# Scaling by the norm after the up projection, and an earlier split of y for w_out, in a float32 block kernel on one core

## The reference

```python
x = x + y                                    # y = concat(...) @ w_o
uf = causal_dwconv(rmsnorm(x, g_ffn[i]) @ w_up[i], w_ffn_conv[i])   # 3 taps over tokens
gate, up = jnp.split(uf, 2, axis=-1)
x = x + (jax.nn.silu(gate) * up) @ w_down[i]

def rmsnorm(x, g):                           # per token t: one factor r[t], per feature: g
    return x * rsqrt(mean(x * x) + 1e-6) * g
```

```python
proj = rms_norm(x, g) @ w_in_2               # q, k, v and gates of the four groups
y = concat(fox, diff, moba, gla) * silu(gates)
x = x + y @ w_out_2
```

## Time and profile before

| | us |
|---|---|
| median of 3 runs | 3679.07 (3676.93 to 3680.88) |
| the profiled execution, its own time | 3682.81 |
| its span, first to last instruction | 3681.0 |
| PE busy in it | 3506.0 (95%) |
| DVE busy | 2588.7 (70%) |
| ACT busy | 1524.9 (41%) |
| POOL busy | 971.7 (26%) |

### The profile page before, as it was taken

How to read it: one execution, slowest core, us unless ns; L and a number is a source line. 1 busy time by engine, 2 the same in 40 slices (tenths; PEclk the granted TensorE clock), 3 DMA queues, 4 the chain that set the end, 5 groups by cost and what they waited for, 6 DMA issues and landing times. The chain is left out here.

```text
span 3681.0 us, 56972 instructions
## 1 busy us (share of the span) xinstructions
PE 3506.0 (95%) x21706; PEld 3093.1 (84%) x21706; DVE 2588.7 (70%) x3400; ACT 1524.9 (41%) x1581; POOL 971.7 (26%) x793
## 2 busy tenths in 40 slices
PE   8988989999999999888899999999999999999998
PEld 7977878888888889877788888888888888878887
DVE  7587577767676765676677676767766866677765
ACT  4432444333433544333444343335444443444442
POOL 3082422212021430553322030313422003140004
PEclk9998999999999999989999999999999999999999
DMA  5332445555555544323455555555543444443443
GB/s 219 138 122 88 152 156 183 174 203 179 198 180 188 190 163 164 133 77 129 150 193 188 188 193 184 193 176 190 177 166 127 150 171 171 166 149 132 155 167 141
DMA packets 93808, 604.06 MB, mean 164 GB/s; under 512 B 10416, under 2 KB 13649, under 8 KB 33105
## 3 DMA queue, kind: packets, MB, share of 16 engines
q1 hardware_dynamic: 92736, 598.78, 46.6%
q10 hardware_dynamic: 912, 3.12, 0.2%
HBM read 599.76 MB, written 2.10 MB: 164 GB/s over the span
## 5 line engine op out<-in xcount | busy, mean ns | idle before, releaser
L531 PE MATMUL bank<-H,whi 128*128 128x512 f32 x6304 | 2247.5, 401 | 44.6 <-DVE H L1444 19.0
L535 PE MATMUL bank<-H,wlo 128*128 128x256 f32 x7552 | 2140.3, 283 | 0.0
L970 ACT ACTIVATE whi<-raw 128x2048 fp32r<-128x2048 f32 (+4 forms) x636 | 1098.5, 1728 | 1180.0 <-DMA raw<-in_slabs_down 274.2
L1364 DVE TENSOR_TENSOR wlo<-raw,whi 128x2048 fp32r<-128x2048 f32 (+4 forms) x636 | 1339.8, 2107 | 250.0 <-ACT whi L970 246.7
L531 PEld LDWEIGHTS bank<-H,whi 128*128 128x128 f32 x6304 | 1192.3, 189 | 343.8 <-issue 37.2
L535 PEld LDWEIGHTS bank<-H,wlo 128*128 128x128 f32 x7552 | 1451.2, 192 | 0.3
L531 PE MATMUL bank<-G,whi 128*128 128x512 f32 x1408 | 488.4, 390 | 0.0
L449 POOL TENSOR_TENSOR sqtmp<-tmp 128x256 f32<-128x256 f32 x88 | 216.6, 2462 | 909.6 <-DVE tmp L1891 909.6
L533 PE MATMUL bank<-H,whi 128*128 128x256 f32 (+1 forms) x1248 | 377.4, 302 | 36.1 <-DVE H L1433 20.9
L535 PE MATMUL bank<-G,wlo 128*128 128x256 f32 x1408 | 397.1, 282 | 0.0
L534 PE MATMUL bank<-H,whi 128*128 128x256 f32 (+1 forms) x1248 | 365.2, 293 | 0.0
(11 more groups left out here) (304 smaller groups left out, 2425.8 us busy)
## 6 DMA issues: line engine op xcount, KB each, us to landing
raw<-in_slabs_up SPq DMA_DIRECT2D x176, 1024.0 KB, 4.8
raw<-in_slabs_down SPq DMA_DIRECT2D x128, 704.0 KB, 4.0
raw<-in_slabs_wo SPq DMA_DIRECT2D x32, 1024.0 KB, 4.8
raw<-in_slabs_pg SPq DMA_DIRECT2D x32, 1024.0 KB, 4.8
raw<-in_slabs_gates SPq DMA_DIRECT2D x32, 1024.0 KB, 4.8
raw<-in_slabs_wout SPq DMA_DIRECT2D x32, 1024.0 KB, 4.8
raw<-in_slabs_ret SPq DMA_DIRECT2D x24, 1024.0 KB, 4.9
raw<-in_slabs_sc SPq DMA_DIRECT2D x24, 1024.0 KB, 4.9
```

Source lines behind the costliest of these rows:

```text
L531: pe.matmul(b[0:r.m, :], whi[:, n % RAW, w], r.src[:, k, :], start=k == 0, stop=False)
L535: last = pe.matmul(b[0:r.m, 0:T], wlo[:, n % RAW, w], r.src[:, k, 0:T], start=False, stop=k == r.kt - 1)
L970: act.activation(whi[:, n % RAW, 0:w], raw[:, n % RAW, 0:w], ACT.Copy).then_inc(S("hi_ready"), 1)
L1364: dve.tensor_tensor(wlo[:, n % RAW, 0:w], raw[:, n % RAW, 0:w], whi[:, n % RAW, 0:w].bitcast(F32), ALU.subtract).then_inc(S("lo_ready"), 1)
```

## The change

Two edits. In up, H is made of x times g without the factor of the norm; `norm_sum` moves behind the first up slab, and DVE multiplies the folded f by `rms` in every up slab. The first four slabs of up(0) are written out ahead of the loop for it (`head`). In front of wout, chunks 0 to 9 of y are split during the last gate slab: ACT and DVE write a quarter of H as soon as PE has read it for the last time (`h_free`), and chunks 12 to 15, 10 and 11 follow ahead of the weight split of s = 60. PE takes the chunks in that order in every wout slab.

```diff
     Y_ORDER = [[12, 13, 14, 15, 4, 5, 6, 7, 0, 1, 2, 3, 8, 9, 10, 11],
-               [12, 13, 14, 15, 0, 1, 2, 3, 4, 5, 6, 7, 8, 9, 10, 11]]
+               [0, 1, 2, 3, 4, 5, 6, 7, 8, 9, 12, 13, 14, 15, 10, 11]]
...
         full = (r.count - tail) // 4 if r.loop else 0
+        for k in range(4 * r.head):
+            yield k // 4, k % 4
         if full >= 2:
-            with eng.Fori(0, full) as i:
+            with eng.Fori(r.head, full) as i:
...
# PE
+                    if key[0] == "gates" and 4 * i + j == r.count - 1 and at in (3, 7, 11):
+                        last.then_inc(S("h_free"), 1)
...
-            norm_sum()
             for g in range(NG + 1):
                 if g < NG:
-                    run(("up", l, g), h_ready(hbase) if g == 0 else None)
+                    run(("up", l, g), h_ready(hbase) if g == 0 else None, norm_beside() if g == 0 else None)
...
-            run(("wout", l), y_ready(hbase, 1))
+            run(("wout", l), y_ready(hbase, 1), order=Y_ORDER[1])
...
# ACT
+            if s == 59:
+                for c in range(10):
+                    act.wait_ge(S("h_free"), 3 * l + c // 4 + 1)
+                    y_split(l, c)
+
+        def y_split(l, k):
+
+            act.wait_ge(S("y_gated"), 16 * l + (k + 5 if k < 10 else k - 9 if k < 14 else k + 1))
+            c = Y_ORDER[1][k]
+            act.activation(H[:, c, 0:T], y[:, c, :], ACT.Copy).then_inc(S("h_hi"), 1)
...
-            norm_h()
+            x_hi("g_ffn", l, "evac", by["wo", l].first)
...
+                        if g == 0 and isinstance(i, int) and i == 0 and j == 0:
+                            norm()
...
-            for k, c in enumerate(Y_ORDER[1]):
-                act.wait_ge(S("y_gated"), 16 * l + k + 1)
-                act.activation(H[:, c, 0:T], y[:, c, :], ACT.Copy).then_inc(S("h_hi"), 1)
+            for k in range(10, 16):
+                y_split(l, k)
...
# DVE, before_split
+            if s == 60:
+                gated(l, 10, 26, 1)
+                gated(l, 11, 27, 1)
+                y_lo(1, 10, 16)
...
# DVE, after_split
-            if s >= 58:
+            if s in (58, 59):
                 gated(l, 8 + s - 58, 24 + s - 58, 1)
-
+            if s == 59:
+                y_lo(1, 0, 10)
...
-            norm_h("g_ffn", l)
+            x_lo("g_ffn", l)
...
-                        link_in_loop(folded(f, b), i, j, 3, 0)
-                        link_in_loop(dve.tensor_scalar(o, f, tap[2], None, ALU.mult), i, j, 3, 1)
+                        if g == 0 and isinstance(i, int) and i == 0 and j == 0:
+                            inverse()
+                        link_in_loop(folded(f, b), i, j, 4, 0)
+                        link_in_loop(dve.tensor_tensor(f, f, rms[:], ALU.mult), i, j, 4, 1)
+                        link_in_loop(dve.tensor_scalar(o, f, tap[2], None, ALU.mult), i, j, 4, 2)
...
-            gated(l, 11, 27, 1)
-            y_lo(1, 0, 16)
             nth("h")
             residual(("wout", l))
```

More of the change, by code:

```diff
@@ L228, in __init__ @@
         self.first = first
+        self.head = 0
 def build(nc, d, out):
@@ L323, in _build @@
         by[key] = Run(d[slab_name(key)], kt, m, count, src, loop, sum(r.count for r in runs))
+        if key[0] == "up" and key[2] == 0:
+            by[key].head = 1
         runs.append(by[key])
@@ L340, in groups @@
         else:
-            full = 0
+            full = r.head
         for k in range(4 * full, r.count):
@@ L508, in nth, with run @@
             return cnt[name]
-        def run(key, operand=None, beside=None, base=None, free=None):
+        def run(key, operand=None, beside=None, base=None, free=None, order=None):
             r = by[key]
@@ L521, in run @@
                 b = bank[n % 4]
-                for k in range(r.kt):
-                    if k == r.kt * 6 // 8:
+                for at in range(r.kt):
+                    k = at if order is None else order[at]
+                    if at == r.kt * 6 // 8:
                         advance(beside, 1)
@@ L526, in run @@
                         within_slab(key[1], base + 4 * i + j)
-                    if operand is not None and (isinstance(i, int) and i == 0 and j == 0 or r.loop and j == 0):
+                    if operand is not None and j == 0 and (i == 0 if isinstance(i, int) else r.loop):
                         operand(k)
@@ L530, in run @@
                     if streams_both(key):
-                        pe.matmul(b[0:r.m, :], whi[:, n % RAW, w], r.src[:, k, :], start=k == 0, stop=False)
+                        pe.matmul(b[0:r.m, :], whi[:, n % RAW, w], r.src[:, k, :], start=at == 0, stop=False)
                     else:
-                        pe.matmul(b[0:r.m, 0:T], whi[:, n % RAW, w], r.src[:, k, 0:T], start=k == 0, stop=False)
+                        pe.matmul(b[0:r.m, 0:T], whi[:, n % RAW, w], r.src[:, k, 0:T], start=at == 0, stop=False)
                         pe.matmul(b[0:r.m, 0:T], whi[:, n % RAW, w], r.src[:, k, T:2 * T], start=False, stop=False)
                     last = pe.matmul(b[0:r.m, 0:T], wlo[:, n % RAW, w], r.src[:, k, 0:T], start=False,
-                                     stop=k == r.kt - 1)
+                                     stop=at == r.kt - 1)
+                    if key[0] == "gates" and 4 * i + j == r.count - 1 and at in (3, 7, 11):
+                        last.then_inc(S("h_free"), 1)
                 last.then_inc(S("slab_done"), 1)
@@ L1001, in y_hi @@
                 act.activation(H[:, c, 0:T], y[:, c, :], ACT.Copy).then_inc(S("h_hi"), 1)
[L1003 to L1006, removed]
         def x_hi(g, l, name, base):
@@ L1406, in invert @@
             dve.reciprocal(inv_rms[:, 0:columns], inv_rms[:, 0:columns]).then_inc(S("inverted"), 1)
[L1408 to L1426, removed]
         def x_lo(g, l):
@@ L1886, in _ @@
                         dve.wait_ge(S("evac"), by["up", l, g].first + 4 * i + j)
-                        link_in_loop(folded(f, b), i, j, 3, 0)
-                        link_in_loop(dve.tensor_scalar(o, f, tap[2], None, ALU.mult), i, j, 3, 1)
+                        if g == 0 and isinstance(i, int) and i == 0 and j == 0:
[3 more added lines that the diff above has]
+                        link_in_loop(dve.tensor_scalar(o, f, tap[2], None, ALU.mult), i, j, 4, 2)
                         link_in_loop(dve.scalar_tensor_tensor(o[:, 1:T], f[:, 0:T - 1], tap[1], o[:, 1:T],
-                                                              ALU.mult, ALU.add), i, j, 3, 2)
+                                                              ALU.mult, ALU.add), i, j, 4, 3)
                         dve.scalar_tensor_tensor(o[:, 2:T], f[:, 0:T - 2], tap[0], o[:, 2:T],
                                                  ALU.mult, ALU.add).then_inc(S("evac"), 1)
-                    loops_end(by["up", l, g], 3)
+                    loops_end(by["up", l, g], 4)
                 if g:
```

## The result

| kernel | median | runs | ratio to the kernel before, 95% interval |
|---|---|---|---|
| before | 3679.98 us | 3676.93 to 3686.47, 4 runs | |
| changed | 3645.03 us | 3637.90 to 3648.13, 4 runs | 0.9900 (0.9879 to 0.9921) |

The account below looks back on a forecast made before the run. PE, busy 95% of the span, was taken as the bound, so only its waits count. Gains of 17.6 + 6.8 + 5.8 + 4.8 = 35.0 us from 3679.1 gave 3644 us, range 3636 to 3663.

Parts of the forecast that it names:

- Part 1: Entries from wo to up: distance falls from 22.63 us to the gla entry's 13.84; 17.6 us gained over both layers.
- The moved norm: Up's first slabs: 8.2 us from slab 0's end until slab 3's low half is there, hidden with 3 us to spare.
- The multiply: Added on DVE in every up slab, 176 in all, 0.42 to 0.94 us each; costs 0 where it meets PE.
- The rival with DVE as the bound: All eight up runs: POOL's reads block DVE; decides from 5.84 us per slab; 3690 us at 6.1; chance 0.05.
- Part 2, layer 1: Entry to wout: PE waits 1.0 us before the eleventh chunk; distance 7.0 us against 13.79, 6.8 gained.
- Layer 0: Entry to wout: 2.0 us wait before the eleventh chunk, distance 8.1 against 14.80; 5.8 us gained, allowing for a possible clock fall.
- Part 3, the pace: Layer 0's up(0) and up(1): PE turns from its slow pace to its fast one, 4.8 us gained.
- layer 1 turns slow: Rival: layer 1's feed-forward, fast before, takes PE's slow pace; 3653.7 to 3663 us; chance 0.13.

Follow-up runs that it names:

- Part 1 alone: The kernel before with only the edit at the entry to up, without the one at wout: 3658.85 us, ratio 0.9949 to the kernel before.
- three multiplies: The changed kernel with the multiply by rms three times in each up slab, not once: 3716.46 us, ratio 1.0089 to the kernel before.
- Two multiplies: The changed kernel with the multiply by rms twice in each up slab, not once: 3650.14 us, ratio 0.9890 to the kernel before.
- no multiply: The changed kernel without the multiply by rms in up: 3642.83 us, ratio 0.9897 to the kernel before.
- eight chunks: The changed kernel with quarters also at three further entries, eight chunks written during the last slab, not twelve or ten: 3629.61 us, ratio 0.9847 to the kernel before.

## Why the prediction was right, and where not

The forecast was 3644 us; the median is 3645.03.

- **Part 1** (17.6 us): 17.9. Taking the distance of the gla entry for that of the up entries was right to 0.4 us (13.48 and 13.91 for 13.84), and x_lo runs 128 times, as forecast. Some of that closeness is luck: in the other profiles with the new entry and the full x_lo behind it the distance is 12.57 to 13.64 us, and that of the gla entry itself, before and after, 12.49 to 13.99. Part 1 alone confirms it with 20.3 us. That profile's own distances, 12.71 and 13.11, account for 19.5.
- **The moved norm**: slab 0 ends at 484.0, slab 3's low half is there at 489.53 + 2.28 = 491.8. That is 7.8 us where the prediction said 8.2, and PE doesn't wait for it. Shown.
- **The multiply**: x176, from 0.42 to 1.01 us with a median of 0.43 over the kernel (forecast 0.42 to 0.94); DVE's wait 0.34 us per slab (forecast some 0.4); its cost to the chain 5.21 - 4.70 = 0.51 us (forecast 0.57 at best). Leaving it out changed the time by less than the runs' spread. The Trainium skill, "SBUF — State Buffer", section "SBUF: two separate sides", has VectorE and GpSimd take the shared ports in turn. The trace of the changed kernel agrees. Of the 176 multiplies 18 take more than 0.6 us, and each of them begins while POOL's L457 is running. Where the multiply begins first, it stays at 0.43 us and L457 takes up to 1.04 instead of 0.74. The other 158 are short, so this seldom matters here. The timeline of POOL and DVE shows one case of each:

```profile
507.58 0.74 POOL L457 TENSOR_TENSOR G<-sqtmp,G 128x256 fp32r<-128x256 f32 x1 [0.53 <-ACT G L1319]
507.75 0.84 DVE L1888 TENSOR_TENSOR tmp<-tmp,rms 128x256 f32<-128x256 f32 x1
...
552.12 0.43 DVE L1888 TENSOR_TENSOR tmp<-tmp,rms 128x256 f32<-128x256 f32 x1
552.13 1.02 POOL L457 TENSOR_TENSOR G<-sqtmp,G 128x256 f32 x1 [0.77 <-ACT G L1319]
```

- **The rival with DVE as the bound** has its mechanism where it was put: three multiplies cost 67 to 71 us. Its threshold of 5.84 us per slab was too high for up(0) and up(1). They follow each other as 44 slabs, not 22, so that the 6.4 us of the prediction make 0.15 per slab and a threshold of 5.70 (an estimate; for up(2) and up(3), with a down run ahead of each, 5.84 stays). Two multiplies at 5.60 lie below both, three at 6.19 above.
- **Part 2, layer 1**: wait 0.82 us (forecast 1.0), distance 6.99 (7.0), gain 6.8 (6.8). **Layer 0**: 7.5 us where 5.8 were forecast. Two terms were too careful: the wait in front of the eleventh chunk was 1.15 and not 2.0 us, because DVE began on the ten chunks at 3034.89, 1.0 us ahead of the end of gates' last slab at 3035.9, where the prediction had 0.2; and the clock did not fall, for which half of 1.7 us had been set aside.
- **Part 3, the pace**, is the step that failed: "The gla entries, where `norm_sum` stands in the stream as it now will here, are followed by the fast one both times. So I expect up(0) and up(1) of layer 0 to run fast". Layer 0 did run fast, by 4.3 us, but in the next profile of the same kernel it was slow, and the kernel before came out fast in its second profile. The premise doesn't hold either: behind the gla entries the pace is the slow one, 353 ns, in three of 24 cases (layer 0 with no multiply, layer 1 with two multiplies and with eight chunks). The pace isn't the change's doing. In the profile after, the rival "layer 1 turns slow" held at the same time (4.7 us lost, up to down(0)), and pg and both wout turned fast (4.9 gained). The term of 4.8 us was met at 4.5 by chance. Without this term the forecast would have been 3649, and with layer 0's 1.7 us more of part 2 and part 1's 0.3, 3647.

The median is right because the entries are; they give 32.2 of the 35 us.

What stays open is what settles the pace. It is not the edit, not the chip, not `norm_sum` in the stream, and not the length of the stall ahead (both paces follow the same 11.4 us). In all profiles but that with three multiplies, the feed-forward from down(0) on ran at 347 ns per chunk, whatever it was before. PE doesn't wait at that place, so "changes only at a disturbance" in the prediction isn't right as a rule.

## What to carry to other kernels

Look for a second place in the kernel that already has the structure the change makes, and take its distance between two instructions whole, with the lower clock in it; that was right to 0.4 us in the first profile and to 1.3 us in all of them, with no sum of parts. When the next product needs the buffer that the last one reads, let the reader free it in quarters and write behind it; the two parts of the gain are starting to write during the last slab and putting the last chunks ahead of the split, and what remains is the writer's own work. An edit worth 5 us in a kernel whose runs spread over 9 to 16 needs the distances in the trace: two profiles can differ by 12 us in stretches that the edit doesn't touch.

## What was not expected of the hardware

- TensorE's pace at granted clock 1.00 has two values for the same pair of matmuls in every stretch without waits that was measured here, 347 and 353 ns: 243 us hold 702 or some 689 pairs. The same stretch of the same program has one value in one execution and the other in the next, also on one chip.
- Behind waits of almost the same length (2.79 and 2.75 us), after the same work, the granted clock stayed at 1.00 once and was 0.59 over the next 4.2 us the other time, in one execution. It cost 1.5 us: the distances are 9.00 and 10.47. The length of a wait near 2.8 us doesn't say alone whether the clock falls.
